# Router logits transposed, the rounded stream stored in column order and read by TensorE with a step of 16 elements, in an encoder layer's mixture-of-experts passage

## The reference

```
h = layer_norm(ALPHA * h + mix, ln1_g, ln1_b)
g_logits = xf @ w_group                      # 4 groups
g_sel    = argmax(g_logits + b_group)
e_logits = (xf @ w_expert)[group g_sel]      # 8 experts of 32
e_local  = top_k(e_logits + e_bias, 2)
e_w      = softmax(e_logits[e_local]) * softmax(g_logits)[g_sel]
y        = (silu(xb @ w1[e]) * (xb @ w3[e])) @ w2[e]      # each expert on its tokens
h = layer_norm(ALPHA * h + sum_k e_w[k] * y[k], ln2_g, ln2_b)
```

## Time and profile before

| | us |
|---|---|
| median of 3 runs | 2152.34 |
| lowest and highest run | 2149.76, 2155.55 |
| span of the profiled execution, first to last instruction | 2148.8 |
| PE busy in it | 2061.8 (96%) |
| DVE busy | 1596.2 (74%) |
| ACT busy | 1276.5 (59%) |

### The profile page before, as it was taken

The page is one execution under the profiler, slowest core; times in us unless marked ns, Lnnn a source line. Parts: engine busy times, 40 slices in busy tenths (PEclk is TensorE's granted clock), DMA queues, the critical chain, the costliest instruction groups (busy, mean ns, idle before and its releaser), DMA issues.

```text
span 2148.8 us, 30033 instructions
## 1 busy us (share of the span) xinstructions
PE 2061.8 (96%) x11484; PEld 1753.2 (82%) x11484; DVE 1596.2 (74%) x1413; ACT 1276.5 (59%) x1060; POOL 106.1 (5%) x77
## 2 busy tenths in 40 slices
PE   8999999999999999999999999999999999999992
PEld 8998888899999998887897778777777777777871
DVE  7646655453737365445668999999999999999997
ACT  5435663333233333333347888888888888888872
POOL 1000000000000000001000000000000000000001
PEclk9999999999999999999999999999999999999996
DMA  6554335655454544557747999999999999999993
GB/s 214 157 138 157 119 128 184 199 180 173 157 161 152 175 154 144 192 195 232 246 196 291 421 421 421 421 421 420 418 420 418 418 421 416 416 415 420 418 409 156
DMA packets 164607, 602.50 MB, mean 280 GB/s; under 512 B 20320, under 2 KB 28656, under 8 KB 113424
## 3 DMA queue, kind: packets, MB, share of 16 engines
q1 hardware_dynamic: 160816, 593.81, 72.7%
q0 software_dynamic: 3712, 7.59, 1.2%
HBM read 595.05 MB, written 18.89 MB: 286 GB/s over the span
## 4 chain that ended last, share of the span: by engine, by line
PE 66%; DVE 16%; issue 7%; DMA 7%; ACT 3%; DVEq 0%; POOLq 0%; POOL 0%; SPq 0%; ACTq 0%
PE ps L1825 19%; PE ps L1806 15%; DVE wl L692 11%; DMA raw<-in_w_dram 7%; PE ps L998 6%; PE ps L999 5%; PE ps L2177 4%; PE ps L995 3%; ACT wh L553 2%; PE ps L1020 2%; PE ps L1931 2%; PE ps L1911 2%; PE ps L1898 1%; DVE yall L843 1%; PE ps L968 1%
## 5 line engine op out<-in xcount | busy, mean ns | idle before, releaser
L692 DVE TENSOR_TENSOR wl<-raw,wh 128x2048 fp32r<-128x2048 f32 x352 | 792.0, 2288 | 42.2 <-ACT wh L553 41.1
L553 ACT ACTIVATE wh<-raw 128x2048 fp32r<-128x2048 f32 x352 | 671.1, 1916 | 140.1 <-DMA raw<-in_w_dram 83.9
L1396 DVE TENSOR_TENSOR wl<-raw,wh 128x2048 fp32r<-128x2048 f32 (+1 forms) x168 | 379.9, 2264 | 283.8 <-ACT wh L1200 283.7
L1200 ACT ACTIVATE wh<-raw 128x2048 fp32r<-128x2048 f32 (+1 forms) x168 | 318.1, 1896 | 443.7 <-DMA raw<-in_w_in_dram 282.2
L998 PE MATMUL ps<-wh,xg 128*128 128x512 f32 x900 | 376.1, 418 | 24.4 <-DVE wl L692 24.1
L999 PE MATMUL ps<-wl,xg 128*128 128x512 f32 x900 | 354.1, 393 | 0.0
L1806 PE MATMUL ps<-hth,wh 128*128 128x272 f32 (+1 forms) x896 | 259.7, 290 | 3.2 <-DVE wl L1396 1.8
L1806 PE MATMUL ps<-htl,wh 128*128 128x272 f32 (+1 forms) x896 | 255.8, 285 | 0.0
L1806 PE MATMUL ps<-hth,wl 128*128 128x272 f32 (+1 forms) x896 | 255.6, 285 | 0.0
L998 PEld LDWEIGHTS ps<-wh,xg 128*128 128x128 f32 x900 | 170.3, 189 | 77.2 <-DVE wl L692 30.3
L998 PE MATMUL ps<-wh,hx 128*128 128x512 f32 x508 | 202.0, 398 | 0.8 <-DVE wl L692 0.8
(11 more groups left out here) (348 smaller groups left out, 3079.2 us busy)
## 6 DMA issues: line engine op xcount, KB each, us to landing
raw<-in_w_dram SPq DMA_DIRECT2D x384, 1024.0 KB, 10.3
raw<-in_w_in_dram SPq DMA_DIRECT2D x103, 1024.0 KB, 5.1
raw<-in_w_pa_dram SPq DMA_DIRECT2D x16, 1024.0 KB, 5.0
raw<-in_w_pb_dram SPq DMA_DIRECT2D x16, 1024.0 KB, 5.0
raw<-in_w_out_dram SPq DMA_DIRECT2D x16, 1024.0 KB, 5.0
raw<-in_w_ukv_dram SPq DMA_DIRECT2D x8, 1024.0 KB, 5.4
yrow<-yscr SPq DMA_DIRECT2D x4, 1024.0 KB, 7.8
raw<-in_w_uq_dram SPq DMA_DIRECT2D x8, 384.0 KB, 3.5
```

The source lines that it names most:

```text
L553: nc.scalar.activation(wh2[:, x % HELD, :], raw2[:, slot2(x), :], ACT.Copy).then_inc(s_wh2, 1)
L692: nc.vector.tensor_tensor(wl2[:, slot2(x), :], raw2[:, slot2(x), :], wh2[:, x % HELD, :].bitcast(F32), ALU.subtract).then_inc(s_wl2, 1)
L1200: nc.scalar.activation(wh[:, n % RING1, 0:c], raw1[:, n % RING1, 0:c], ACT.Copy).then_inc(s_wh, 1)
L1396: nc.vector.tensor_tensor(wl[:, n % RING1, 0:c], raw1[:, n % RING1, 0:c], wh[:, n % RING1, 0:c].bitcast(F32), ALU.subtract).then_inc(s_wl, 1)
```

## The change

- `logits` uses the router weights (36 columns) as the stationary operand and 256 tokens as the moving one: 16 float32 matmuls of 256 columns. ACT copies the result (36 x 256) to `lgt`, PE transposes it back in two pieces, and DVE reads these.
- `xh1` and `xl1` are kept in the order of the stream's own columns. ACT, DVE and the last addition (line 892) read and write them in a row. PE's gathers read a block as 128 elements with a step of 16 elements (64 bytes).
- Unit 0 is no longer split; PE reads it whole.
- `stream_rest` of both tiles comes after the ranks and `s_mxr`. Of the first gathers, q = 0 to 6 come before unit 0, and q = 7 behind it.
- `keep_warm` is spread differently: 2, 24, five times 3 behind steps of DVE's routing chain, 3, and twice 4, where it was 36 and 16.
- The softmax weights are made in two parts: up to the exponentials' inputs at k = 3, the rest at k = 10; ACT's exponentials come at k = 9. In the first pair, the selection moves from k = 8 to 11, and the first expert's hidden layer (sigmoid, product, mix) from k = 12 to 14.

```diff
-        xh1 = place("xh1", [P, TT, KD, P], 98304, F32R)
-        xl1 = place("xl1", [P, TT, KD, P], 114688, F32R)
+        xh1 = place("xh1", [P, TT, D_MODEL], 98304, F32R)
+        xl1 = place("xl1", [P, TT, D_MODEL], 114688, F32R)
...
-            return (24 - len(XR)) * (turn + x // 24) + X_SPLIT[x % 24]
+            return (24 - len(XR)) * (turn + x // 24) + X_SPLIT[x % 24] - 1
+        def whole(turn, x):
+            return x % 24 in XR or (isinstance(turn, int) and 24 * turn + x == 0)
...
+        def block_of(stream, t, k):
+            return stream[:, t, :].rearrange("q (p k) -> q k p", k=KD)[:, k, :]
...
         def scalar_experts(act):
             def hi(turn, x):
-                if x % 24 in XR:
+                if whole(turn, x):
                     return
...
+                    if k == 14 and early:
+                        sigmoid(2 * turn)
                     hi(turn, x + HELD)
-                    if k == 3 and early:
+                    if k == 9 and early:
                         early()
...
-                    if k == 12:
+                    if k == 12 and not early:
                         sigmoid(2 * turn)
...
-            hi(0, 0)
             hi(0, 1)
             for t in range(TT):
                 act.wait_ge(s_h1, t + 1)
-                nc.scalar.activation(xh1[:, t, :, :], mrg[:, t, :].rearrange("q (p k) -> q k p", k=KD),
-                                     ACT.Copy).then_inc(s_xh1, 1)
+                nc.scalar.activation(xh1[:, t, :], mrg[:, t, :], ACT.Copy).then_inc(s_xh1, 1)
...
             def stream_rest(t):
                 dve.wait_ge(s_xh1, t + 1)
-                nc.vector.tensor_tensor(xl1[:, t, :, :], mrg[:, t, :].rearrange("q (p k) -> q k p", k=KD),
-                                        xh1[:, t, :, :].bitcast(F32), ALU.subtract).then_inc(s_xl1, 1)
+                nc.vector.tensor_tensor(xl1[:, t, :], mrg[:, t, :], xh1[:, t, :].bitcast(F32), ALU.subtract).then_inc(s_xl1, 1)
             def lo(turn, x):
-                if x % 24 in XR:
+                if whole(turn, x):
                     return
...
                 own.after(nc.vector.tensor_reduce(top, tmp, AXX, ALU.min))
+                routed.append(own.count)
...
-                                                   ps[:, t, 0:G + E], ALU.mult, ALU.add)
+                                                   ps[:, 1, (G + E) * t:(G + E) * (t + 1)], ALU.mult, ALU.add)
             own.after(s)
+            routed.append(own.count)
...
             own.after(nc.vector.tensor_tensor(r1[:, :, :], el, brt[:, G:G + E].unsqueeze(1).broadcast_to([P, TT, E]), ALU.add))
+            routed.append(own.count)
...
             dve.wait_ge(s_asg, 1)
-            stream_rest(0)
...
-            stream_rest(1)
+            for t in range(TT):
+                stream_rest(t)
             for x in range(HELD):
                 lo(0, x)
-            def combine_weights():
+            def exponents():
...
+            def combine_weights():
                 dve.wait_ge(s_mxt, 1)
...
-                    if k == (8 if first else 5):
+                    if k == (11 if first else 5):
                         select(turn, p)
...
+                    if k == 14 and early:
+                        hidden(2 * turn, 0, turn)
                     lo(turn, x + HELD)
-                    if k == 3 and early:
-                        early()
+                    if k in (3, 10) and early:
+                        early[k == 10]()
...
-                    if k == 12:
+                    if k == 12 and not early:
                         hidden(2 * turn, 0, turn)
...
-            one_round(0, 1, early=combine_weights)
+            one_round(0, 1, early=(exponents, combine_weights))
...
-                s = nc.vector.tensor_tensor(acc[:, t, :].rearrange("q (p k) -> q k p", k=KD), xh1[:, t, :, :].bitcast(F32),
-                                            xl1[:, t, :, :].bitcast(F32), ALU.add)
+                s = nc.vector.tensor_tensor(acc[:, t, :], xh1[:, t, :].bitcast(F32), xl1[:, t, :].bitcast(F32), ALU.add)
...
             for j in range(4):
                 logits(j)
-            keep_warm(36)
+            keep_warm(2)
+            pe.wait_ge(s_lgc, 1)
+            for t in range(TT):
+                m = nc.tensor.transpose(ps[:, 1, (N_GROUPS + N_EXP) * t:(N_GROUPS + N_EXP) * (t + 1)],
+                                        lgt[:, P * t:P * (t + 1)], ident[0:N_GROUPS + N_EXP, 0:N_GROUPS + N_EXP])
+            m.then_inc(s_lg, 1)
+            keep_warm(24)
+            for step_ in routed:
+                pe.wait_ge(s_dve, step_)
+                keep_warm(3)
             pe.wait_ge(s_asg, 1)
...
             def gather(g, q, *waits):
...
-                            m = nc.tensor.matmul(bank[:, b, :, h, :], src[:, t, 2 * q + b, :],
+                            m = nc.tensor.matmul(bank[:, b, :, h, :], block_of(src, t, 2 * q + b),
...
-            def first_gather(q, h):
+            def first_gather(q, h, tiles_):
...
-                    if early and k < 4:
-                        if k == 1:
-                            first_gather(4, 1)
-                            first_gather(5, 1)
-                        if k == 2:
-                            for q in (6, 7):
-                                pe.wait_ge(s_xg, q - 5)
-                                first_gather(q, 0)
-                                first_gather(q, 1)
                         pe.wait_ge(s_xg, 2 * k + 2)
...
+                    if early and k == 0:
+                        pe.wait_ge(s_xg, 1)
+                        for h in range(2):
+                            first_gather(7, h, (0, 1))
...
-                    if k == 12:
+                    if k == (14 if early else 12):
                         mix(turn, j, 0, (s_hp, j) if last else (s_xg, 8 * (turn + 1) + 4))
...
-            keep_warm(16)
+            keep_warm(3, 0)
             pe.wait_ge(s_pg, 1)
             pe.wait_ge(s_mxr, 1)
             pe.wait_ge(s_xh1, TT)
-            for q in range(6):
-                first_gather(q, 0)
-            pe.wait_ge(s_xl1, TT)
-            for q in range(4):
-                first_gather(q, 1)
+            for q in range(7):
+                first_gather(q, 0, (0, 1))
+            for t in range(TT):
+                keep_warm(4, 0)
+                pe.wait_ge(s_xl1, t + 1)
+                for q in range(7):
+                    first_gather(q, 1, (t,))
...
             for j in range(4):
                 turned(j)
+            act.wait_ge(s_lgt, 1)
+            nc.scalar.activation(lgt[:, :], ps[0:N_GROUPS + N_EXP, 0, 0:SEQ], ACT.Copy).then_inc(s_lgc, 1)
             scalar_experts(act)
...
             def logits(j):
                 pe.wait_ge(s_ytc, j + 1)
-                for t in range(TT):
-                    for b in range(4 * j, 4 * j + 4):
-                        m = nc.tensor.matmul(ps[:, t, 0:N_GROUPS + N_EXP], yt[:, b, P * t:P * (t + 1)], gwr[:, b, :],
-                                             start=b == 0, stop=b == KD - 1, skip_group_check=True)
+                for b in range(4 * j, 4 * j + 4):
+                    m = nc.tensor.matmul(ps[0:N_GROUPS + N_EXP, 0, 0:SEQ], gwr[:, b, :], yt[:, b, :],
+                                         start=b == 0, stop=b == KD - 1, skip_group_check=True)
                 if j == 3:
-                    m.then_inc(s_lg, 1)
+                    m.then_inc(s_lgt, 1)
```

More of the change, by code:

```diff
@@ L307, in moe_trunk @@
         b1t = place("b1t", [P, KD], 202048)
+        lgt = place("lgt", [N_GROUPS + N_EXP, SEQ], 199680)
         gwr = place("gwr", [P, KD, N_GROUPS + N_EXP], 202112)
@@ L362, in moe_trunk @@
         s_xl1 = sem("s_xl1")
+        s_lgt = sem("s_lgt")
+        s_lgc = sem("s_lgc")
         s_lg = sem("s_lg")
@@ L430, in moe_trunk @@
         G_AT = (4, 6, 8, 10, 16, 18, 20, 22)
-        FIRST_BANK = (7, 6, 5, 4, 3, 2, 7, 6)
+        FIRST_BANK = (7, 6, 5, 4, 3, 2, 1, 7)
         G_FIRST = (8, 9, 10, 11, 16, 18, 20, 22)
         LAST_BANK = (0, 1, 6, 7)
+        routed = []
         def sync_experts(sp):
@@ L943, in tensor_experts, with keep_warm @@
                 turn_stream(j)
-            def keep_warm(count):
+            def keep_warm(count, bank=4):
                 for _ in range(count):
-                    nc.tensor.matmul(ps[:, 4, 0:P], ones[:, :], ident[:, :], start=True, stop=True, skip_group_check=True)
+                    nc.tensor.matmul(ps[:, bank, 0:P], ones[:, :], ident[:, :], start=True, stop=True, skip_group_check=True)
             for j in range(4):
                 logits(j)
-            keep_warm(36)
+            keep_warm(2)
[8 more added lines that the diff above has]
+                keep_warm(3)
             pe.wait_ge(s_asg, 1)
@@ L971, in gather @@
                 m.then_inc(s_gt, 1)
-            def first_gather(q, h):
+            def first_gather(q, h, tiles_):
                 bank = ps[:, FIRST_BANK[q], :].rearrange("p (k a h s) -> p k a h s", k=2, a=2, h=2)
```

(8 more changed lines are left out.)

## The result

The changed kernel takes 2213.3 us (median of 4, 2210.7 to 2217.3) against 2152.2 before: 1.029 times as long, interval 1.0277 to 1.0302. The forecast was 2226. The profiled execution has a span of 2211.3.

What follows compares the result with a forecast made beforehand. DMA weight streaming was taken as the bound, PE 3% behind. Stepped loads beyond PE's reserve (73.4), + 5.3 later unit 0, + 1.4 whole unit, - 1.1 gathers, - 5.1 stall gave + 74: 2226 us, whole range 2143 to 2244.

Steps and rivals of the forecast that it cites:

- The stepped load: PE's gathers in the expert stage: 0.225 us a load instead of 0.105, 0.84 exposed a group, 101 us over 120 groups.
- The reserve: PE's idle time in the DMA-bound expert stage, 27.6 us, which hides that much added PE work.
- the stall: After unit 0, PE starves while ACT waits for the exponentials' inputs; its 5.1 us of idling were to go.
- The passage: Logits, ranks, splits and first gathers before the expert stage: ranks read at 1118.7, unit 0 starting near 1134.5, 5.3 later.
- rival D: PE's clock falls to half pace in the first gathers, adding up to 10 us; inside the range, no chance given.
- the DMA share in the stage: Sign in the expert stage: 0.94 if the forecast is right, 1.01 if the stepped load costs PE nothing.
- Rival A: Gathers: the stepped load costs PE nothing, DMA stays the bound; 2147 us, between 2143 and 2152; chance 0.38.
- B: Gathers: a small price, up to 0.033 us a load, hidden by PE's idle time; about 2150 us; chance 0.06.
- C: Gathers: a price well over two, 0.42 us a load, 265 us in place of 101; near 2390; chance 0.03.

Runs made afterwards that it cites:

- e1_block: The changed kernel with the rounded stream back in block order, so PE reads neighbouring elements: 2147.0 us, ratio 0.998 to the kernel before.
- e5_order: The kernel before with the column order alone, PE stepping by 16 elements: 2220.1 us, ratio 1.032 to the kernel before.
- e3_step4: The changed kernel with the stream stored in fours, PE reading with a step of 4 elements (16 bytes): 2231.4 us.
- e4_half: The changed kernel with only the high halves in column order and the low halves in block order: 2160.9 us, ratio 1.004 to the kernel before.
- e9_step8: The changed kernel with the stream stored in eights, PE stepping by 8 elements (32 bytes): 2241.3 us in one run.
- e2_step2: The changed kernel with the stream stored in pairs, PE stepping by 2 elements (8 bytes): 2144.9 us, ratio 0.9968 to the kernel before.
- e6_split: e2_step2 with unit 0 split again as in the kernel before: 2145.6 us, ratio 0.998 to the kernel before.
- e8_high_only: e1_block with the expert stage's gathers of the low halves left out: 2163.9 us, ratio 1.006 to the kernel before.

## Why the prediction was right, point by point

**The stepped load**, the deciding term, was right in kind and near in size. I had 0.225 from ACT's and DVE's rows and a group dearer by 0.84; measured are 0.22 and 0.76 (1.60 - 0.84). 120 x 0.76 = 91 us where the text has 101. The 0.105 of a load in a row was the step that made it too large: it shares the 0.84 among eight, but the first load is partly hidden, and inside a gather the starts lie 0.112 apart in block order and 0.219 stepped. The steps of 2 and 4 elements put the break between 8 and 16 bytes, where a new 16-byte line with each element would put it. The rule on SBUF lines in the Trainium skill (Advanced Engine Details and Errata, SBUF Cachelines), that full speed needs two hits on a line, agrees with 0.88 against 1.69 us a gather. The Trainium skill's rule of columns alone (TensorE: Matmul & The Clock Gate, LDWEIGHTS) does not hold here for stepped reads of float32: 128 columns take 0.105 or 0.22.

**The reserve** was 27.6 plus the 5.1 of the stall. The same sum from the kernel before, span against span, is 91 + 9.6 (later end of unit 0) - 0.5 (gathers left after it) - 62.5 = 38 hidden. Mis-sized by 5. It is a remainder of that sum, but the runs against `e1_block`, where the stall is mostly gone (PE idles for 2.5 of 40 us), fit it: 33 to 34 hidden, and `e1_block` is 4.6 us faster than before. So the reserve alone was 33 to 34, not 27.6. A likely part of the difference, which no run tries apart, is that the rows that I scaled leave out that PE's clock fell twice for 3.4 us in the stage of the kernel before (from 1153.0 and 2067.8), which is 3.4 us of work, and it never does between 1138.7 and 2150 in the changed kernel.

**The passage** came as laid out: logits 7.10 (7.2), ranks read at 1118.70 (1118.7, though this execution comes to the passage 0.6 later, so that they are 0.6 sooner than laid out), gathers from 1120.08 (1120.0), splits 4.49 / 2 = 2.25 (2.23). Only the end was later, unit 0 at 1135.85 instead of 1134.5, and 5.09 long instead of 3.5. That is rival D, which happened: the clock fell in the stepped first gathers here, in `e3_step4`, `e4_half`, `e5_order` and `e9_step8`, and neither in `e1_block` nor in `e2_step2` (with pairs it did once, for 3.4 us, in `e6_split`). It cost 3, not 10, since a stepped load keeps its pace at 0.50 (below) and only the idle matmuls and unit 0 became longer: 1.67 instead of 0.95 twice, and 5.09 instead of 3.5.

Together: 91 for 101, 38 hidden for 33, 3 for the clock. The 74 become 62.5. The forecast is 13 us too high because the group and the reserve are mis-sized the same way, and the clock takes back only 3.

**What failed** is one sign that I named: the DMA share in the stage was to be 0.94 and is 0.99. The share counts the time in which transfers are under way, and for the same bytes they are under way longer: 0.99 for 392 GB/s against 1.01 for 418. **Rival A** is what `e1_block` is, 2147 as priced there; its step costs nothing because it has none. B and C are out. The stall's 5.1 were booked to the moved softmax work and the fewer gathers, and PE's idle time is indeed gone (0.3 of 40 us). But `e5_order`, without these edits, idles for only 1.9 where before idles for 4.7, so more than half of it goes without them once PE is late.

## What to carry to other kernels

A step that one engine has to take is cheapest where a longer operation covers it: here the 128-column gathers had no cover, while 512-column matmuls cover all but 0.010 us of a load. Before a reordering is moved from one engine to another, compare layouts that keep two float32 side by side; here they were nearly as good as rows for all three engines (PE 0.88 for 0.84 us a gather, ACT 1.92 for 1.85 and DVE 2.24 for 2.25 a split). And a DMA share near 1 does not say that DMA is the bound: read the GB/s beside it, and which engine the weights' first consumer waits for.

## What the runs showed of the hardware

A stepped load keeps its pace when PE's clock is halved. In the changed kernel 28 of them take 1126.30 - 1120.08 = 6.22, 0.222 each, mostly at 0.50, and 0.22 each in the stage at 1.00. Loads in a row take 3.16 / 28 = 0.113 in `e1_block` at 1.00, and 3.03 / 14 = 0.216 in `e4_half` at 0.50:

```profile
1119.44 3.31 PE L1004 MATMUL ps<-pg,xh 128*128 128x128 f32 x28 [0.73 <-DVE pg L760]
1122.60 1.10 PE L964 MATMUL ps<-ident,ones 128*128 128x128 f32 x8
```

```profile
1128.11 3.23 PE L1004 MATMUL ps<-pg,xl 128*128 128x128 f32 x14
1131.14 2.02 PE L964 MATMUL ps<-ident,ones 128*128 128x128 f32 x8
```

So the step costs as much as half the clock, and the two don't add up. With 0.22 / 128 = 1.7 ns an element for PE beside the 1.79 of ACT and 1.72 to 1.83 of DVE, a limit on the memory's side fits all three; that it lies there is inferred, not shown. The second surprise is `e8_high_only`: PE was given less to do beside the stream of weights, it idled, its clock fell to 0.50 once in every turn of the loop, and the kernel ended 17 us later. Which of these caused the delay stays open.
